# GpSimd's token and weight sums of a gated DeltaNet layer cut into pieces of one contraction block, and some evacuations moved in VectorE's and ScalarE's order

## The reference

```python
proj = h @ w_in                       # columns: q, k, v of 8 heads, gates b and a, memory query, z
qkv, b, a, qm, z = split(proj)
conv = silu(sum(xpad[:, wi:wi + T] * conv_w[wi] for wi in range(4)))   # short causal conv
q, k, v = split(conv)                 # per head; q and k are L2-normalised
beta, g = sigmoid(b), -exp(a_log) * softplus(a + dt_bias)
# chunked delta rule, per head: lmat = strict_lower(kb @ k.T * decay), solved for u and w,
# then chunk by chunk: v_new = u - w @ S; o = qg @ S + aqk @ v_new; S = S * exp(gl) + kdec.T @ v_new
o, S = gated_delta(q, k, v, g, beta, S0)
branch = concat([rmsnorm(o), mem_attend(qm, mem_k, mem_v)]) * silu(z)
x = x + branch @ w_out
```

## Time and profile before

| | before |
|---|---|
| median of three runs | 2258.49 us |
| the profiled execution's own time | 2256.38 us |
| its span (first to last instruction) | 2254.3 us |
| TensorE matmul busy | 2151.9 us (95%), 19742 instructions |
| VectorE busy | 1025.5 us (45%), 2494 instructions |
| ScalarE busy | 665.2 us (30%), 1596 instructions |
| GpSimd busy | 629.0 us (28%), 740 instructions |
| groups 0 to 15 of layer B | about 1140 to 1780 us of the span |

### The profile page before, as it was taken

The page is one execution under the profiler, slowest core; times in us unless marked ns, Lnnn a source line. Parts: engine busy times, 40 slices in busy tenths (PEclk is TensorE's granted clock), DMA queues, the critical chain, the costliest instruction groups (busy, mean ns, idle before and its releaser), DMA issues.

```text
span 2254.3 us, 47365 instructions
## 1 busy us (share of the span) xinstructions
PE 2151.9 (95%) x19742; PEld 1563.9 (69%) x19742; DVE 1025.5 (45%) x2494; ACT 665.2 (30%) x1596; POOL 629.0 (28%) x740
## 2 busy tenths in 40 slices
PE   8999999999999999999898898898899999999998
PEld 6888888888888875544566676676676666665444
DVE  5243444454354453312366666667666323333252
ACT  4122211312312222211233333333344344452101
POOL 0512232232232132001436546546443020010000
PEclk9999999999999999999999999999999999999999
DMA  7412211401212276672111111211101163015451
GB/s 226 159 34 77 57 40 29 111 24 48 75 38 68 58 235 230 210 245 81 29 62 60 64 74 66 68 76 69 55 38 41 31 236 133 19 45 170 133 175 54
DMA packets 210280, 211.02 MB, mean 94 GB/s; under 512 B 14261, under 2 KB 181653, under 8 KB 209150
## 3 DMA queue, kind: packets, MB, share of 16 engines
q1 hardware_dynamic: 198070, 148.27, 21.9%
q0 software_dynamic: 12000, 59.73, 7.0%
HBM read 179.56 MB, written 68.23 MB: 110 GB/s over the span
## 4 chain that ended last, share of the span: by engine, by line
PE 41%; POOL 5%; DVE 3%; issue 2%; DMA 1%; ACT 1%; POOLq 0%; DVEq 0%; ACTq 0%
PE bank L3045 8%; PE bank L2133 8%; PE bank L3535 7%; PE bank L2183 6%; PE bank L2243 3%; PE bank L2259 2%; DVE arena L2693 2%; POOL arena L2938 1%; PE bank L2241 1%; POOL arena L2889 1%; DMA arena<-in_w_in_b 1%; POOL arena L2903 1%; PE bank L2251 1%; PE bank L3061 1%; PE bank L3070 1%
## 5 line engine op out<-in xcount | busy, mean ns | idle before, releaser
L884 PE MATMUL bank<-arena 128*128 128x256 f32 (+1 forms) x2688 | 631.7, 386 | 0.0
L884 PEld LDWEIGHTS bank<-arena 128*128 128x128 f32 x2688 | 494.5, 190 | 75.3
L2183 PE MATMUL bank<-arena 128*128 128x264 f32 x784 | 241.1, 420 | 3.4 <-ACT arena L2422 3.0
L2133 PE MATMUL bank<-arena 128*128 128x352 f32 x624 | 220.4, 473 | 0.1
L3045 PE MATMUL bank<-arena 128*128 128x352 f32 x576 | 176.4, 459 | 0.0
L1338 POOL TENSOR_TENSOR arena<-arena 128x272 f32<-128x272 f32 (+1 forms) x48 | 31.4, 654 | 507.9 <-ACT arena L1058 487.9
L3535 PE MATMUL bank<-arena 128*128 128x512 f32 x360 | 167.5, 599 | 0.0
L2259 PEld LDWEIGHTS bank<-arena 32*32 32x32 f32 x7680 | 81.0, 107 | 117.6 <-issue 40.3
L2183 PEld LDWEIGHTS bank<-arena 128*128 128x128 f32 x784 | 135.6, 198 | 21.1 <-ACT arena L2422 3.4
L2259 PE MATMUL bank<-arena 32*32 32x16 f32 (+1 forms) x7680 | 99.7, 184 | 46.7 <-DVE arena L2697 30.3
L3045 PEld LDWEIGHTS bank<-arena 128*128 128x128 f32 x576 | 106.6, 190 | 53.3
(11 more groups left out here) (440 smaller groups left out, 2936.3 us busy)
## 6 DMA issues: line engine op xcount, KB each, us to landing
arena<-in_w_in_a SPq DMA_DIRECT2D x48, 512.0 KB, 5.2
arena<-in_w_in_b SPq DMA_DIRECT2D x40, 512.0 KB, 5.8
arena<-in_cache_win_k SPq DMA_DIRECT2D x48, 256.0 KB, 4.8
arena<-in_cache_win_v SPq DMA_DIRECT2D x48, 256.0 KB, 3.6
out<-arena SPq DMA_DIRECT2D x40, 256.0 KB, 3.4
arena<-in_w_mem_kv SPq DMA_DIRECT2D x16, 512.0 KB, 8.1
arena<-in_cache_mem_k SPq DMA_DIRECT2D x32, 256.0 KB, 4.1
arena<-in_cache_mem_v SPq DMA_DIRECT2D x32, 256.0 KB, 3.6
```

What stands on the lines that cost most here:

```text
L884: m = nc.tensor.matmul(o[:, 0:hi - lo], w, y, start=k == 0 and i in (0, 1, 3, 5), stop=k == KH - 1, skip_group_check=i in (2, 4, 6))
L2133: m = nc.tensor.matmul(o[:, 0:PART], ring.slots[:, (B1 + b) % RING, k, :], part_in(k, part_), start=k == 0, stop=k == KD - 1)
L2183: m = nc.tensor.matmul(o[:, 0:QUART], w, y, start=k == 0 and i in (0, 1, 3, 5), stop=k == KH - 1, skip_group_check=i in (2, 4, 6))
```

## The change

- `token_sums` does each sum as four instructions of 128 x 264, one for each contraction block, in place of one of 128 x 1056. `weight_sums` does each as two of 128 x 256 (two blocks each) in place of one of 128 x 512. The semaphore is counted by the last piece.
- `SUMS_AT` gets entries for slots 0 to 3: the ends of slots 0, 1 and 2 would be dealt with in slot 3.
- ScalarE and VectorE evacuate the first half of a slot's units ahead of the chunk's step. VectorE evacuates the second half directly behind the chunk's step, so ahead of the norm's inverses, the factors and the conv step of the slot, which it had done first. ScalarE's second half keeps its place.
- Ahead of group 0, GpSimd's first token and weight sums come behind the prefixes and the memsets, and directly ahead of `squares(0)`.

```diff
-    SUMS_AT = {9: (), 10: (), 11: (), 12: (), 13: (9, 10, 11, 12, 13)}
+    SUMS_AT = {9: (), 10: (), 11: (), 12: (), 13: (9, 10, 11, 12, 13), 0: (), 1: (), 2: (), 3: (0, 1, 2, 3)}
...
 (ScalarE)
+                beside(units_at(G, s, 0))
                 if G and s in RSLOT:
                     chunk_step(G - 1, s)
                 if G == NG_ and s == 15:
                     out_roots(NG_ - 1)
-                beside(units_at(G, s))
+                beside(units_at(G, s, 1))
...
 (VectorE)
+                beside(units_at(G, s, 0))
                 if G and s in RSLOT:
                     chunk_step(G - 1, s)
+                beside(units_at(G, s, 1))
                 if s == AT_INV:
...
                     conv(G + 2, *conv_at[G % 2][s])
-                beside(units_at(G, s))
...
 (GpSimd, weight_sums)
-                nc.gpsimd.tensor_tensor(*v).then_inc(tws, 1)
+                for p0 in (0, KH // 2):
+                    x = nc.gpsimd.tensor_tensor(*(y[:, p0:p0 + KH // 2, :] for y in v[:3]), v[3])
+                x.then_inc(tws, 1)
...
 (GpSimd, token_sums)
-                nc.gpsimd.tensor_tensor(*v).then_inc(ttk, 1)
+                for k in range(KH):
+                    x = nc.gpsimd.tensor_tensor(*(y[:, k, :] for y in v[:3]), v[3])
+                x.then_inc(ttk, 1)
...
 (GpSimd, ahead of group 0)
         nc.gpsimd.memset(xpad[:, :, 0:CW - 1], 0.0).then_inc(xzero, 1)
-        token_sums(0, range(4))
-        weight_sums(1, range(4))
         pool.wait_ge(cvi, 1)
         for i in range(3):
             prefix(0, i)
         pool.wait_ge(gev, 2)
         for k in range(1, LEVELS - 2):
             nc.gpsimd.memset(X[k], 0.0).then_inc(xzero, 1)
+        token_sums(0, range(4))
+        weight_sums(1, range(4))
         squares(0)
```

## The result

The change made the kernel slower: 2273.09 us (median of four runs, 2270.14 to 2278.5) against 2257.62 us of the kernel before, a ratio of 1.007 [1.0051, 1.0089]. The forecast was 2261 us with a range up to 2273, which the median passes by 0.1 us; what came true is the rival "GpSimd becomes the bound outright". The profiled execution is the slowest of the four, 2278.5 us around a span of 2276.4, 22.1 us above the span before. Its trace therefore shows some 5 us that the median does not have.

The account below looks back on a forecast made before the run. TensorE was taken to set the pace, waiting on VectorE and GpSimd's copy-load round. Lateness of 1.5 us at the end plus 1 for the clock gave 2258.9; the median 2.1 above it made 2261 us, range 2243 to 2273.

Parts of the forecast that it names:

- GpSimd becomes the bound outright: Rival: upper bounds hold, lateness about +13 us, clock up to +4: 2275 us, half of that 2267; chance 0.35.
- ring: GpSimd's two-group round of 84.89 us: copy, load, sums, samples, line 2946, sums, copy; total slack 12.3 us.
- Pieces, what they cost GpSimd: GpSimd's token and weight sums: pieces and handovers to VectorE make each round 2.1 us longer, against 0 to 4.3 slack.
- the first copy: GpSimd's first cache copy: 1.8 us later, from four token sums (1.2) and handovers (0.6) ahead of it.
- the slack: GpSimd's idle time before line 2946: 2.82, 4.29, 2.36, 2.4, 0.42 us in groups 3 to 11, none in group 1.
- the clock: TensorE's fallen clock behind waits moved to slots 6 and 13: partly hidden, 1 us added.
- From line 2946 to the copy: Stretch of GpSimd's round with four token sums: 4 x 0.3 = +1.2 us, bounds 0 and 1.8.
- From load to line 2946: Stretch of GpSimd's round with four weight and two token sums: +0.9 us, bounds 0 and 1.9.
- handover: GpSimd letting VectorE in oftener between pieces: some 0.1 us each, +0.3 (0 to 0.6) from load to line 2946.
- Behind the last ring: After group 11 no sum is left and TensorE runs on, so 1.5 us of lateness reach the end.
- copy to first weight sum: Sign in GpSimd's timeline that the forecast is right: this distance stays at 43 us.
- Relief wins: Rival: pieces cost GpSimd next to nothing, 2245 us; if also the load didn't hang on the copy, 2227; chance 0.27.

Follow-up runs that it names:

- e6: The changed kernel without layer B's 12 early cache copies, their output rows left out: 2234.38 us, 0.9907 of the kernel before.
- e5: The kernel before without layer B's 12 early cache copies, their output rows left out: 2222.65 us, ratio 0.9852.
- e1: The kernel before with token sums in four pieces and weight sums in two, nothing else of the change: 2270.0 us against 2256.34, ratio 1.0058.
- e4: The kernel before with only the token sums in pieces, weight sums whole: 2267.19 us against 2256.34, ratio 1.0046.
- e2: The kernel before with only the first token and weight sums moved behind prefixes and memsets, sums whole: 2255.2 us against 2256.34, ratio 0.9996.
- e3: The kernel before with only the new order of ScalarE's and VectorE's evacuations: 2258.45 us against 2256.34, ratio 1.0012.
- e9: The kernel before with both copies of each pair of groups issued in the odd group's slot 1, behind the pair's loads: 2232.03 us against 2255.81, ratio 0.9898.
- e7: The kernel before with even groups' copies issued in slot 9 of GpSimd's program instead of slot 1, all copies made: 2335.32 us, ratio 1.0353.
- e8: The changed kernel with even groups' copies issued in slot 9 instead of slot 1, all copies made: 2255.32 us, 1.0003 of the kernel before.

## Why the prediction was wrong

The mechanism was right: a ring through copy and load that pieces lengthen. The step that failed is "Pieces, what they cost GpSimd", in its size: I had 2.1 us for each ring, and it measured 3.1. Three other terms were off the same way, the first copy, the slack and the clock. Worked out from the trace of after, ring by ring:

- *From line 2946 to the copy* I had +1.2, bounds 0 and 1.8. Measured: +2.15, 1.89, 1.87, 1.89, 1.69, above the upper bound four times out of five. The four token sums in it cost 0.43 each where VectorE is quiet, the upper bound of 0.45 and not the +0.3 taken, and 0.97 where it is let in. In group 7 the first two take 1.95 us more, the last two 0.85 more, and the squares between them 0.91 less, which had taken 2.90 us and take 1.99: together the 1.89.
- *From load to line 2946* I had +0.9, bounds 0 and 1.9. Measured, idle time taken off: +0.74, 1.00, 1.09, 1.63, 2.47, 0.53, on average 1.24. The weight sums in it depend on what runs beside them: three of them are 5.04 us in pieces and 4.40 whole in group 7 of the two kernels, but 4.83 and 4.99 in e6 and e5. Between e1 and e4 they are worth 2.8 us, and the intervals of the two overlap.
- So a ring costs some 3.1 us and not 2.1, just what the rival named as its turning point ("above some 3 us"). Five rings, with the -0.4 that copy to load gave in them, are 16.0 us where I had 10.5. The step was wrong in how it priced a piece. One row of a 264-wide add, start to start 0.61 us, stood for all four sums. The pieces have two durations, 0.64 and 0.74 us, by which sum they belong to (the whole sums too: two of the four take 2.40 us at the least, the other two 2.05), and a piece beside which one of VectorE's conv steps runs takes up to 1.20, the most in the durations above; 51 of the 52 pieces over 1 us have such a step beside them. The whole sum pays for being let in once, its pieces several times. My 0.1 for a handover came from no row. Its 0.3 for the whole stretch from load to line 2946 was too little, and behind line 2946 I charged none: 0.97 less 0.43 is 0.54 per sum beside the conv.
- *First copy:* +1.8 forecast, +5.34 measured (1145.13 against 1139.79), just above the upper bound of 5. The four token sums ahead of it took 2.0 us more, about as worked out; the other 3.4 us were there at line 2946 already, where I had 0. The 16 pieces at the start took 14.75 us where 9.8 + 3.6 = 13.4 were worked out (the 0.4 us for each conv step let in came from no row either), and TensorE's norms came 2.5 us later, bound +2. As an edit by itself the moved start costs nothing, as forecast (e2).
- *Slack:* I let the lateness eat all of it, 11.9 us in groups 1 to 9. Only 8.5 of 11.8 were given: TensorE, which also arrives later, brings line 2946's operand late in its turn, and 0.24, 2.20 and 0.89 us of idle time stay in groups 1, 5 and 7. My sum also let the lateness at line 2946 fall below 0 in groups 5, 7 and 9, as if TensorE came early there; held at 0 it would have been 1.2 late at the copy of group 10 instead of 0.4. Measured there: 5.34 + 16.0 - 8.5 = 12.86 late.
- *Behind the last ring:* I let nothing grow once the sums are over. In the trace the 12.86 us become 13.85 at line 2946 of group 11, 18.25 at line 2946 of group 12, and 22.1 at the end. Between groups 11 and 12 TensorE idles 1.0 us more than before and loses 3.4 us more to the clock; from there to the end it is 2.9 and 2.0.
- *The clock:* I added 1 us. It lost 12.0 us more than before over all of layer B, in 17 stretches instead of 10, mostly behind short waits in slot 6 and slot 13 that earlier came as one long wait in slot 3. This too was in the rival's text ("if the clock falls"), but at up to 4 us. So the rival's 2275 is near the median of 2273.09 in part by luck: its 13 us of lateness came true, its 4 us for the clock did not, and the execution that I could take apart is itself 5.4 us above the median. How much of it follows the waits and how much makes them isn't separated by these runs.

What held: the table's entries do nothing; the order of evacuations is near nothing (+2.1 us in e3's median, a ratio of 1.0012 [1.0002, 1.0022], just clear of none); line 2693's four instructions take 2.46 to 3.33 us in the odd groups 3 to 11 (about 3 forecast); the wait for 2697 falls to 1.3 to 2.3 us there, 1.7 on average (2.2 forecast); copy to first weight sum stays (42.6 to 47.4 us, 42.9 to 47.7 before); the time moves to 2717 and 2724. The rule of the Trainium skill, SBUF — State Buffer, section "Who interferes with whom", that the other engine is blocked for a whole instruction, agrees with 6.58 us whole and 2.46 in pieces. The rule names no price for the engine that lets the other in at every gap; here that is 0.54 us per token sum, and it is GpSimd's loss.

The estimate from the Trainium skill, GPSIMD Engine Reference, section 3.1, had 0.06 us of fixed cost per instruction. The quiet pair shows (5.46 - 4.61) / 6 = 0.14 us for each further instruction, so here the measurement decides against it.

"Relief wins" fell on the first of its two conditions, that pieces cost GpSimd next to nothing (0.43 us for each token sum in e6 where VectorE is quiet); on the second it was right in kind. Loads that don't hang on the copy are worth 24 us with the copies made (e9) and 34 without them (e5); I gave 32 for such a load together with the pieces. But it isn't the pieces that free it, it is the order of two issues.

## What to carry to other kernels

When work is cut into pieces so that a second engine gets in, price the piece from the engine that is cut, once alone and once with the other engine let in, and add it up along that engine's own chain until its next deadline; the shorter wait that one looks at is the smaller half of the sum. Where an engine sits in a ring with a transfer, look first whether the transfer's order of issue can be changed: e9's edit changes two lines and wins 24 us. And place a DMA relative to the DMA it must not precede, not by a slot of an engine that may run ahead of it.

## What the runs showed of the hardware

- A 512 KB load on SP's queue, issued 0.86 us behind a 2 MB copy from HBM to HBM that GpSimd issued, lands 43.2 us after its issue, about when the copy does (43.0 us after its own). Issued 1.01 us ahead of it, it lands after 4.0 us and holds nobody up (e7, e8). In the kernel before it is issued 19.4 us behind the copy and takes 23.4 us, and the copy 41.5.
- GpSimd's f32 adds: 128 x 264 take 0.64 or 0.74 us, four pieces of a 128 x 1056 sum 2.73 against 2.30 whole where VectorE does little beside them (e6, e5). Beside VectorE's conv the pieces are 3.41 each sum against 2.45 whole. Two pieces of 128 x 256 take 1.41 us and one sum of 128 x 512 takes 1.31, at 1462.01 us of the changed kernel and 1450.08 of the one before.
- Many short waits of TensorE can cost more clock than few long ones: 77.6 us of idle time in the changed kernel came with 17 stretches at 1.2 GHz and 42.7 us lost, 70.0 us in the one before with 10 stretches and 30.7. Each number is of one execution.
